# A hybrid encoder layer: the decays of a head formed one head ahead, A ahead of the attention matrix, and the block inverse, its transfers and the scan three positions later

## The reference

```
G = cumsum(g)                                        # log decays within a chunk
decay = exp(where(i >= j, G[i] - G[j], -inf))
A = where(i > j, beta[i] * (k k^T) * decay, 0)
T = inverse(I + A)
u = T (beta v);  w = T (beta exp(G) k)
attn = (q k^T) * decay
per chunk: v_new = u - w S;  o = (q exp(G)) S + attn v_new
           S = S exp(G_last) + (k exp(G_last - G))^T v_new
o = rmsnorm(o) * silu(z)
```

## Time and profile before

| | us |
|---|---|
| median of 3 runs | 1406.68 |
| lowest, highest | 1402.7, 1409.77 |
| profiled execution, its own time | 1399.55 |
| its span, first to last instruction | 1397.8 |

### The profile page before, as it was taken

How to read it: one execution, slowest core, us unless ns; L and a number is a source line. 1 busy time by engine, 2 the same in 40 slices (tenths; PEclk the granted TensorE clock), 3 DMA queues, 4 the chain that set the end, 5 groups by cost and what they waited for, 6 DMA issues and landing times.

```text
span 1397.8 us, 20307 instructions
## 1 busy us (share of the span) xinstructions
PE 1170.5 (84%) x7486; PEld 1038.1 (74%) x7486; DVE 752.1 (54%) x1090; ACT 555.1 (40%) x732; POOL 122.7 (9%) x164
## 2 busy tenths in 40 slices
PE   4987997988979799798887999971888988888870
PEld 4987997988979799798887999971555555555550
DVE  4437265463654636536365454335666666666635
ACT  4423232232333323233241222250666666666632
POOL 0012030020300203003020000004000000000002
PEclk9999898998989989899898999985899999999995
DMA  5273232222222323323213235534988999999936
GB/s 175 83 252 99 76 97 67 82 79 82 94 81 81 88 71 89 88 68 90 76 42 107 90 103 170 219 129 165 324 308 329 324 319 327 326 324 324 329 104 220
DMA packets 82361, 227.16 MB, mean 163 GB/s; under 512 B 22090, under 2 KB 40146, under 8 KB 70034
## 3 DMA queue, kind: packets, MB, share of 16 engines
q1 hardware_dynamic: 41538, 194.32, 40.8%
q10 hardware_dynamic: 36704, 17.02, 4.3%
q0 software_dynamic: 4080, 15.30, 3.3%
HBM read 191.68 MB, written 34.94 MB: 162 GB/s over the span
## 4 chain that ended last, share of the span: by engine, by line
PE 65%; DVE 12%; DMA 11%; ACT 6%; issue 4%; POOL 1%; ACTq 1%; SPq 0%; DVEq 0%; POOLq 0%
PE proj L672 20%; PE proj L1404 15%; PE wideB L1425 7%; PE proj L1054 5%; DMA ablk<-scr_a 3%; DVE prod L518 3%; PE wideB L406 2%; DMA T<-scr_t 2%; PE proj L997 2%; PE wideA L1391 2%; DVE xbl L1493 2%; DVE tblk L522 2%; PE wideA L412 2%; DMA wraw<-in_w_in 2%; ACT xbh L1489 2%
## 5 line engine op out<-in xcount | busy, mean ns | idle before, releaser
L672 PE MATMUL proj<-xnh,whi 128*128 128x288 f32 x1152 | 351.5, 305 | 13.9 <-DVE xnl L1942 7.2
L672 PE MATMUL proj<-xnh,wlo 128*128 128x288 f32 x1152 | 352.7, 306 | 0.0
L672 PE MATMUL proj<-xnl,whi 128*128 128x288 f32 x1152 | 350.9, 305 | 0.0
L672 PEld LDWEIGHTS proj<-xnh,whi 128*128 128x128 f32 x1152 | 223.1, 194 | 15.7 <-DVE ubuf L781 6.9
L1481 DVE TENSOR_TENSOR elo<-eraw,ehi 128x4096 fp32r<-128x4096 f32 x64 | 214.5, 3353 | 19.7 <-ACT ehi L1471 19.6
L672 PEld LDWEIGHTS proj<-xnl,whi 128*128 128x128 f32 x1152 | 223.7, 194 | 0.0
L672 PEld LDWEIGHTS proj<-xnh,wlo 128*128 128x128 f32 x1152 | 223.4, 194 | 0.2
L1404 PE MATMUL proj<-ehi,xbh 128*80 128x512 f32 x256 | 111.4, 435 | 34.0 <-DVE xbl L1493 34.0
L684 DVE TENSOR_TENSOR wlo<-wraw,whi 128x1024 fp32r<-128x1024 f32 x72 | 92.9, 1290 | 62.7 <-ACT whi L680 62.7
L1471 ACT ACTIVATE ehi<-eraw 128x4096 fp32r<-128x4096 f32 x32 | 116.0, 3625 | 0.4
L1404 PE MATMUL proj<-elo,xbh 128*80 128x512 f32 x256 | 109.8, 429 | 0.0
(11 more groups left out here) (313 smaller groups left out, 2066.1 us busy)
## 6 DMA issues: line engine op xcount, KB each, us to landing
wraw<-in_w_in SPq DMA_DIRECT2D x72, 512.0 KB, 3.6
eraw<-in_w_gate SPq DMA_DIRECT2D x32, 1024.0 KB, 5.1
eraw<-in_w_up SPq DMA_DIRECT2D x32, 1024.0 KB, 7.6
eraw<-in_w_down SPq DMA_DIRECT2D x32, 1024.0 KB, 5.6
wraw<-in_w_out SPq DMA_DIRECT2D x24, 512.0 KB, 4.0
xb<-scr_rows SPq DMA_DIRECT2D x32, 320.0 KB, 6.2
scr_y<-yout SPq DMA_DIRECT2D x32, 320.0 KB, 5.8
grow<-scr_row POOLq DMA_DIRECT2D x8, 640.0 KB, 6.9
```

Source lines behind the costliest of these rows:

```text
L672: mm = pe.matmul(out, w[:, kc, :], x[:, kc, hh * HALF:(hh + 1) * HALF], start=(j == 0), stop=(j == 23))
```

## The change

The subtraction, the first mask, the exponential and the second mask move out of `gdn_pool` and out of p = 3 of ACT into a part of their own, `decay_pool` and `decay_scalar`. They are done for the next head: POOL's part stands behind the loads at the end of `gdn_pool`, with a copy of five columns (`gsum`) that it needs, and ACT's exponential stands at p = 30, ahead of the rest of the delta rule there. For head 0 both stand ahead of the first joint round, on POOL behind the load of its row, on ACT ahead of everything of that round. DVE forms `aT` at p = 4 and `attnT` at p = 5, ACT issues the transfer of `aT` at p = 5 instead of 7 and of `ablk` at p = 8 instead of 9. `SOLVE0` goes from 11 to 13, and with it the write of the blocks (16 to 18) and their read (19 to 21); `LEVEL0` goes from 22 to 25, and with it the levels, the scan and the norm.

```
-        LEVEL0 = 22
-        SOLVE0 = 11
+        LEVEL0 = 25
+        SOLVE0 = 13
+        EXP_AT = 30
...
+        def decay_scalar(act, g):
+            act.wait_ge(s["dstep"], 3 * g + 3)
+            act.activation(decay[:, :], decay[:, :], ACT.Exp).then_inc(s["decay_set"], 1)
...
+            if p == EXP_AT and not last:
+                decay_scalar(act, n)
...
-            if p == 3:
-                act.wait_ge(s["dclip"], n)
-                act.activation(decay[:, :], decay[:, :], ACT.Exp).then_inc(s["decay_set"], 1)
-            if p == 7:
+            if p == 5:
                 act.wait_ge(s["a_set"], n)
                 act.dma_start(unit_blocks(scr_a), units(aT[:, :])).then_inc(s["a_out"], 16)
-            if p == 9:
+            if p == 8:
...
+        def decay_pool(pool, g):
+            n = g + 1
+            pool.tensor_copy(gsum[:, :], dec[:, KSUM, at(g), :].rearrange("p a u -> p (a u)"))\
+                .then_inc(s["dstep"], 1)
+            pool.wait_ge(s["dstep"], 3 * g + 1)
+            pool.wait_ge(s["row_in"], 16 * n)
+            wait(pool, s["attn_set"], g)
+            pool.tensor_tensor(units(decay[:, :]), units(grow[:, 0, :]),
+                               gsum[:, :].unsqueeze(2).to_broadcast([P, UNITS, P]), ALU.subtract)\
+                .then_inc(s["dstep"], 1)
+            pool.wait_ge(s["dstep"], 3 * g + 2)
+            pool.tensor_tensor(units(decay[:, :]), units(decay[:, :]), causal_mask, ALU.mult).then_inc(s["dstep"], 1)
+            pool.wait_ge(s["decay_set"], n)
+            pool.tensor_tensor(units(decay[:, :]), units(decay[:, :]), causal_mask, ALU.mult)\
+                .then_inc(s["decay_cut"], 1)
...
             row_load(pool, 0)
+            decay_pool(pool, 0)
             proj_pool(pool, 1)
             gdn_pool(pool, 0)
+            late_pool(pool, 0)
...
                 if p == ROWS_AT:
                     rows_scalar(act)
+            decay_scalar(act, 0)
             act.wait_ge(zero_out, 64)
```

More of the change, by code:

```diff
@@ L185, in encoder_layer @@
         dec = sb(gd, "dec", [P, KINDS, HEADS, UNITS])
+        gsum = sb(gd, "gsum", [P, UNITS])
         gcur = sb(gd, "gcur", [P, KINDS, UNITS])
@@ L400, in gdn_tensor @@
                     if k == 0:
-                        pe.wait_ge(s["t_in"], 16 * n)
-                        pe.wait_ge(s["tt_in"], 16 * n)
+                        pe.wait_ge(s["t_in"], 32 * n)
                     else:
@@ L454, in gdn_tensor, with gdn_scalar @@
                 mm.then_inc(s["o_turned"], 1)
-        def gdn_scalar(act, p, g):
+        def decay_scalar(act, g):
+            act.wait_ge(s["dstep"], 3 * g + 3)
+            act.activation(decay[:, :], decay[:, :], ACT.Exp).then_inc(s["decay_set"], 1)
+        def gdn_scalar(act, p, g, last=False):
             n = g + 1
+            if p == EXP_AT and not last:
+                decay_scalar(act, n)
             if p == 0:
@@ L547, in gdn_vector @@
                    .then_inc(s["vn_set"], 1)
-            if p == 5:
+            if p == 4:
                 dve.wait_ge(s["grams"], n)
-                dve.wait_ge(s["decay_cut"], n)
-                dve.tensor_tensor(units(attnT[:, :]), gram[:, :, 0, :], units(decay[:, :]), ALU.mult)\
-                   .then_inc(s["attn_set"], 1)
-            if p == 6:
                 dve.wait_ge(s["decb_set"], n)
@@ L556, in gdn_vector @@
                    .then_inc(s["a_set"], 1)
+            if p == 5:
+                dve.tensor_tensor(units(attnT[:, :]), gram[:, :, 0, :], units(decay[:, :]), ALU.mult)\
+                   .then_inc(s["attn_set"], 1)
             if SOLVE0 <= p < SOLVE0 + 5:
@@ L621, in gdn_pool @@
                 .then_inc(gdec_set, 1)
-            pool.wait_ge(gdec_set, n)
-            pool.wait_ge(s["row_in"], 16 * n)
-            pool.tensor_tensor(units(decay[:, :]), units(grow[:, 0, :]), spread(KSUM), ALU.subtract)\
-                .then_inc(s["dgap"], 1)
-            pool.wait_ge(s["dgap"], n)
-            pool.tensor_tensor(units(decay[:, :]), units(decay[:, :]), causal_mask, ALU.mult).then_inc(s["dclip"], 1)
             pool.wait_ge(conv_silu, 3 * g + 2)
             pool.tensor_tensor(qg[:, :], sil[:, 0, :], grow[:, 1, :], ALU.mult).then_inc(s["qg_set"], 1)
-            pool.wait_ge(s["decay_set"], n)
-            pool.tensor_tensor(units(decay[:, :]), units(decay[:, :]), causal_mask, ALU.mult)\
-                .then_inc(s["decay_cut"], 1)
             pool.wait_ge(s["decay_cut"], n)
@@ L642, in gdn_pool, with late_pool @@
                 row_load(pool, g + 1)
+        def late_pool(pool, g):
+            decay_pool(pool, g + 1)
         def half_read(h, i):
@@ L1835, in _ @@
                 gdn_pool(pool, i - 1)
+                late_pool(pool, i - 1)
                 tails_pool(pool, i, 0)
@@ L1918, in _ @@
                     fill_scalar(act, p)
-                gdn_scalar(act, p, HEADS - 1)
+                gdn_scalar(act, p, HEADS - 1, last=True)
                 if p > 0:
```

6 lines of the change are left out of this document (3 added, 3 removed).

## The result

| | before | after |
|---|---|---|
| median | 1399.52 us | 1414.49 us |
| lowest, highest | 1390.72, 1470.62 | 1402.81, 1417.66 |
| profiled execution, its own time | 1399.55 | 1415.78 |
| its span | 1397.8 | 1414.1 |

There are 20 runs of each. One run of before (1470.62 us) is slow and left out of the ratio; the next longest took 1409.77. The ratio of after to before is 1.0089, with a 95% interval of 1.0063 to 1.0114: the change makes the kernel about 12.5 us slower (the two medians lie 15.0 us apart). The time that I had named is the median of after, and that is luck: part of the way there was another one, as the traces show.

A forecast was written before the change was run, and what follows sets the result against it. Each head was taken to be bound by the landing of T plus PE's remaining work. Terms -25.6 + 14.9 + 6.3 + 9.1 + 4.0 - 0.9 = +7.8 us on 1406.7 gave 1414.5 us, range 1400 to 1423.

The forecast's parts named there:

- (1) Cover: PE's wait for T: three more projection positions ahead of it in each of 8 heads, -25.6 us.
- (2) The solve ends later: DVE's solve, heads 0 to 6: waits for the fifth tile's split, which needs ACT's whi; +14.9 us.
- Nothing: List of parts forecast to cost nothing, among them POOL's decay parts, said to fall where DVE idles.
- (3) The load of SP: SP's 512 KB weight load shares transfer engines with the read of T: +6.3 us in seven heads (0 to 9.8).
- the sign that I gave: Among the signs that would show the forecast right: the read of T lands in 4.4 to 5 us.
- (4) The exponential: ACT at p = 30: table load and exponential delay the TT copy before level 3; +9.1 us (5 to 13).
- my fourth rival: A drain with each table switch: 1.38 us more at the TT copy in seven heads, 1424 us; chance 0.03.
- (5) Head 0: First joint round: ACT waits for POOL's mask, so the squares end later; +4.0 us (3 to 6.5).
- (6) Head 7: Head 7's end: later norm, longer waits, against a filler-split collision gone and earlier T; -0.9 us (-2 to +1.5).
- that waits give way to the cover: Faster rival: ACT's whi comes before the blocks of A, the exponential before its copy; 1388.6 us, chance 0.14.
- that no transfers collide: No-change rival: SP's load costs nothing and the exponential its lower bound; about 1403 to 1410 us, chance 0.24.
- more held up: Slower rival: load and exponential at upper bounds, head 0 at the lower clock; 1426 us, chance 0.11.

The follow-up runs named there:

- e4: Kernel before with LEVEL0 = 25 instead of 22 and nothing else; 1376.11 us (0.9861 times before).
- e1: Changed kernel with SOLVE0 = 12 instead of 13, the solve one position earlier, ahead of the fifth tile's split; 1396.11 us (0.9996 times before).
- e10: Changed kernel with SOLVE0 = 11, EXP_AT = 31 and 28 unread transposes on PE ahead of the router; 1374.38 us (0.9827 times before).
- e5: Changed kernel with DVE's split of the sixth weight tile moved from position 18 to 22; 1419.32 us (1.0124 times before).
- e2: Changed kernel with EXP_AT = 31 instead of 30, the exponential behind ACT's copy of TT; 1412.55 us (1.0081 times before).
- e12: Kernel before with 28 unread transposes on PE ahead of the router's first wait; 1397.11 us.
- e7: Changed kernel with 28 unread transposes on PE ahead of the router's first wait; 1403.86 us.
- e3: Changed kernel with head 0's exponential on ACT moved behind the two squares of position 0; 1418.51 us (1.0108 times before).
- e8: Changed kernel with 56 unread transposes on PE (28 in head 7) ahead of the wait for T; 1408.45 us.
- e6: Changed kernel with SOLVE0 = 12, EXP_AT = 31 and DVE's split of the sixth tile at position 24; 1391.06 us (0.9911 times before).
- e11: Changed kernel with 80 unread transposes (40 in head 7) ahead of the wait for T and 28 ahead of the router; 1379.58 us (0.9852 times before).
- e9: Kernel before with LEVEL0 = 25 and 28 unread transposes on PE ahead of the router; 1377.15 us (0.983 times before).

## Why the prediction came out as it did

The forecast was +7.8 us. Up to the merge the traces give +3.5; with the router's clock taken out, the runs give +6 to +6.7; with it, about +12.5 by the ratio and +15.0 by the medians. The direction was right. That the time named (1414.5) is the median to a tenth is luck: two errors of 7 us cancel. The median of the three runs that I started from was 7.2 us above that of the twenty, and by the medians the change cost 7.2 us more than my sum, about what the router's clock adds (8), for which I had no term.

**(1) Cover.** Right. From the third level to the next products it takes 37.65 us in after, 3.04 less than before, 21.3 us in seven heads; e4 shows the whole of it as time.

**(2) The solve ends later.** Right in cause and size. In heads 0 to 6 the solve starts at 15.64 and ends at 26.7 to 26.9 behind the products, where 15.6 and 26.8 stood. Over seven heads the solve's end moved by 15.4 us; the sum had 14.9. e1 takes the split away, and the rows start 3.2 us earlier.

One thing under "Nothing" was wrong: POOL's parts of the decay do not fall where DVE idles. They come 7.6 to 11.1 us behind the products, beside the convolution, and make it end 2.2 us later. In after this is hidden behind the wait for `whi`, and DVE's idle time ahead of the split is 1.95 us instead of the 4.2 that I had worked out. In e1 and e10 it is not hidden: the solve starts straight behind the convolution. No run moves POOL's part away, so what that would give is not shown.

**(3) The load of SP.** Right in size, wrong in place. From the solve's end to PE it was 7.7 us more in seven heads, against 6.3. But I had the load collide with the read of `T`. It met the write of the blocks, 0.17 us ahead of it, which took 3.9 us instead of the 2.0 of e5; the read then had the way free and took 3.1 instead of 3.8. So the sign that I gave, a read of 4.4 to 5 us, did not show. e5 puts the load on the read and gets 5.5 us, which is 2.4 more than the read alone, well over my upper bound of 1.4. That bound took 3.8 us for a read alone; with the 3.1 of after it would have been 1.9, still too low.

**(4) The exponential.** The wait came as foreseen, 7.1 us in seven heads with the table load right behind the split, and e2 ends it. From the second level to the third it takes 1.2 us more a head (7.17 instead of 5.96), 8.2 in seven heads, against 9.1. But the time from the first level to the third rose by only 1.8 us in seven heads together, not by 9.1, because the clock came back earlier: the second level started 8.9 us behind the first in after (10.7 in head 6), and 10.5 to 10.8 in five heads of before. Head 4 of before:

```profile
491.28 2.39 PE L406 MATMUL wideB<-T,aT 128*128 128x64 f32 x10 [9.10 <-DMA T<-scr_t]
...
502.05 1.22 PE L406 MATMUL wideB<-T,aT 128*128 128x64 f32 x10
```

It is no accident of these two traces: e12 and e7, with the same code in the heads, have 10.6 to 11.0 in five heads, and 8.4 to 8.8 in six. The failed step is my worked head. Head 3 of before is, with head 2, one of two in which the clock came back some 5 us behind PE's start, where it took about 10 in the other five; I took its rows for typical, and had no term for the clock.

No drain of the kind in my fourth rival stands in front of the table load, which follows the split 0.01 us behind. The Trainium skill (ScalarE: Activation LUTs, What ACT_TABLE_LOAD costs) adds one to each switch of sets; the trace does not bear that out here.

**(5) Head 0.** +4.1 us for +4.0, with a wait of 3.3 us for the squares. e3 shows that the reason was only half told: POOL's order holds the head as much as ACT's. The lower clock that I had feared there came in e3, behind a wait of 4.88 us, and not in after.

**(6) Head 7.** It gave back 4.0 us, cover and ends together, where 4.1 stood; PE's wait for `ybl` is 2.67 us for a forecast of 2.6.

**Behind the heads** I had nothing. PE's start of the merge was 3.5 us late, and the longer wait for `ybl` leaves the clock low for the first matmuls of the merge (0.44 us each instead of 0.29), 1.5 us. The router stage took 10 us more at 1.2 GHz. e7 shows that this is the clock: with PE kept busy ahead of it the stage takes 11.3 us. Which kernels get it I cannot say: e1, e4, e8 and before had the stage at full rate in the profiled execution, after, e2, e3, e5 and e6 had not, and after has both among its runs. The idle time ahead of the stage is 4.1 us in all. What decides whether the clock comes back there stays open.

The rivals: that waits give way to the cover fell with (2); that no transfers collide fell with (3); "more held up" (1426) was not reached. No drain showed, as said under (4).

## What to carry to other kernels

Where a wait is long enough for TensorE's clock to fall, count the work behind the wait at the lower clock too, and over all heads, not in one that was worked out: a microsecond taken from the wait may come back as slower matmuls behind it, and filling the wait with work on PE can be worth as much as shortening it. By the start of head 7's products the filling gave 18 us (e11 against e7), the solve one position earlier 8 (e1), and `T` 4.8 us earlier 28 (e10 against e7); the filling and the earlier `T` together were not run. When a step moves in an order written by hand, look at what its neighbours on the same engine wait for: a split that was harmless between the rows held up the solve ahead of them, and POOL's work, moved to where DVE seemed idle, slowed the convolution. And test the parts of a change alone: the one number `LEVEL0` gave 23 us, and the rest of the change took 38 away, some 11 of them by way of the router's clock (e7 and e9, both with the router at full rate, lie 27 us apart).

## What the runs showed of the hardware

- PE at work does not always bring the clock back soon. In the levels of the runs without transposes in the wait for `T` it came back 4 to 12 us behind PE's start (4.0 in head 1 of e10, 11.6 in its head 6), and in the router stage of after not at all in 25 us of unbroken work. The Trainium skill (TensorE: Matmul & The Clock Gate, HAM oscillation) tells of PE falling back to half rate in each wait for data and starting the next piece there; the levels of every head of before and after agree, with 0.50 at PE's start on `T`. The 25 us of the router stage, with no wait in them, are not what it describes.
- Transposes that nothing reads keep the clock up: with at most 1.0 us of idle time left it stayed at 1.00 (e11), with 2.5 to 3.6 us left it fell (e8, heads 0 to 6).
- A 512 KB load of SP costs about 2 us to a small transfer that is under way with it: the write of the blocks 3.9 instead of 2.0 us, the read of `T` 5.5 instead of 3.1.
- Transposes in a row start 0.109 us apart at the full clock, in the 56 of e8 as in the groups of 8 of the router stage. A group of 8 takes 1.07 us, 0.133 for each, only because the last one's 0.27 us count in full. From that 0.133 I had sized the first filling of the wait, and so it fell short.
- Steps of DVE's convolution (128x579) take 0.82 us each alone and 1.70 and 2.01 beside POOL's subtraction and mask of 128x640. In e10, where POOL's part comes 0.7 us later, it is the second and third step that take 1.70 and 2.02.
